# Up matrices of chunks 2 to 4 in seven half-block products, with the third weight sum made by an adding transfer

## The reference

```
h = rmsnorm(x, norm_mix[i]);  x = x + mixer_i(h)
h = rmsnorm(x, norm_mlp[i])
a = relu(h @ w_up)            # 512x1024 @ 1024x4096
x = x + (a * a) @ w_down      # 512x4096 @ 4096x1024
...
return rmsnorm(x, norm_final)
```

## Time and profile before

| | |
|---|---|
| median of 3 runs | 1083.18 us (1082.9 to 1083.55) |
| profiled execution | 1082.86 us, its span 1081.1 us |
| granted TensorE clock | 0.997 of full speed |
| PE busy | 1068.0 us, 99% |
| DVE busy | 723.8 us, 67% |
| ACT busy | 508.4 us, 47% |
| POOL busy | 81.5 us, 8% |

### The profile page before, as it was taken

How to read it: one execution, slowest core, us unless ns; L and a number is a source line. 1 busy time by engine, 2 the same in 40 slices (tenths; PEclk the granted TensorE clock), 3 DMA queues, 4 the chain that set the end, 5 groups by cost and what they waited for, 6 DMA issues and landing times.

```text
span 1081.1 us, 13565 instructions
## 1 busy us (share of the span) xinstructions
PE 1068.0 (99%) x5224; PEld 886.2 (82%) x5224; DVE 723.8 (67%) x1221; ACT 508.4 (47%) x839; POOL 81.5 (8%) x143
## 2 busy tenths in 40 slices
PE   9999999999999999999999999999999999999996
PEld 8888888988888888888877777779888888888884
DVE  5886788676576576578426666535775675675687
ACT  6132256663463463466424444326663463463453
POOL 3480000000000000000110000000000000000000
PEclk9999999999999999999999999999999999999998
DMA  7993235235335335310454333152235235235011
GB/s 239 388 376 108 78 80 187 85 79 175 98 78 176 98 77 175 100 40 20 135 164 134 107 93 96 60 233 78 79 82 192 78 79 193 79 78 195 1 40 78
DMA packets 32672, 133.19 MB, mean 123 GB/s; under 512 B 5280, under 2 KB 5408, under 8 KB 26848
## 3 DMA queue, kind: packets, MB, share of 16 engines
q1 hardware_dynamic: 20448, 69.25, 19.2%
q0 software_dynamic: 12160, 63.07, 18.9%
HBM read 113.80 MB, written 10.48 MB: 115 GB/s over the span
## 4 chain that ended last, share of the span: by engine, by line
PE 98%; DVE 1%; ACT 0%; issue 0%; DVEq 0%; POOL 0%; POOLq 0%; ACTq 0%
PE bank L446 31%; PE bank L448 30%; PE bank L447 30%; PE bank L599 2%; PE bank L581 1%; PE bank L566 1%; PE bank L469 1%; PE bank L614 0%; DVE xs L983 0%; ACT big L749 0%; DVE big L1029 0%; DVE w_l L927 0%; PE bank L636 0%; PE bank L632 0%; DVE big L1249 0%
## 5 line engine op out<-in xcount | busy, mean ns | idle before, releaser
L446 PE MATMUL bank<-a_h,w_h 128*128 128x512 f32 (+1 forms) x896 | 337.3, 377 | 0.1
L448 PE MATMUL bank<-a_h,w_l 128*128 128x512 f32 (+1 forms) x896 | 335.2, 374 | 0.0
L447 PE MATMUL bank<-a_l,w_h 128*128 128x512 f32 (+1 forms) x896 | 335.1, 374 | 0.0
L446 PE MATMUL bank<-w_h,hx 128*128 128x512 f32 x568 | 222.0, 391 | 0.0
L448 PE MATMUL bank<-w_h,hx 128*128 128x512 f32 x568 | 221.0, 389 | 0.0
L447 PE MATMUL bank<-w_l,hx 128*128 128x512 f32 x568 | 221.0, 389 | 0.0
L721 ACT ACTIVATE w_h<-raw 128x1024 fp32r<-128x1024 f32 x115 | 121.3, 1058 | 174.9 <-PE bank L448 142.9
L927 DVE TENSOR_TENSOR w_l<-raw,w_h 128x1024 fp32r<-128x1024 f32 x115 | 139.7, 1220 | 92.0 <-PE bank L448 63.1
L446 PEld LDWEIGHTS bank<-a_h,w_h 128*128 128x128 f32 x896 | 168.7, 188 | 32.5 <-issue 3.1
L448 PEld LDWEIGHTS bank<-a_h,w_l 128*128 128x128 f32 x896 | 168.7, 188 | 30.2
L447 PEld LDWEIGHTS bank<-a_l,w_h 128*128 128x128 f32 x896 | 168.8, 188 | 29.8 <-issue 0.2
(11 more groups left out here) (112 smaller groups left out, 806.0 us busy)
## 6 DMA issues: line engine op xcount, KB each, us to landing
raw<-weights SPq DMA_DIRECT2D x116, 512.0 KB, 3.5
big<-blocks POOLq DMA_DIRECT2D x36, 1024.0 KB, 5.1
big<-big POOLq DMA_DIRECT2D x9, 1024.0 KB, 8.0
bias_tiles<-big POOLq DMA_DIRECT2D x8, 624.0 KB, 9.5
big<-bias_tiles POOLq DMA_DIRECT2D x8, 624.0 KB, 4.1
bias_tiles<-bias_rows POOLq DMA_DIRECT2D x48, 64.0 KB, 12.4
big<-x SPq DMA_DIRECT2D x8, 256.0 KB, 4.7
raw<-wave SPq DMA_DIRECT2D x8, 256.0 KB, 5.0
```

What stands on the lines that cost most here:

```text
L446: nc.tensor.matmul(dst, sh, mh, start=start, stop=False, skip_group_check=again)
L447: nc.tensor.matmul(dst, sh, ml, start=False, stop=False, skip_group_check=again)
L448: return nc.tensor.matmul(dst, sl, mh, start=False, stop=stop, skip_group_check=again)
```

## The change

Six of the eight up matrices (chunks 2 to 4 of each MLP) are computed by a new function `up_seven`, in seven products of half blocks. The weight part stays in the array (stationary) and 256 tokens of the activations move, so that the result keeps the features on the partitions. A product is 14/7 = 2 units, each 4 output slices x 2 slices x 3 matmuls of 256 columns. Now 15 matrices of weights go through blocks (`MATRIX`), 1 + 2 x 7.

- The sums of the input's blocks are made once per MLP from `a_h` and `a_l`: `in_sums` on VectorE in units 5 to 7 of the first up matrix and in products 3 and 4 of the first down matrix, `in_round` on ScalarE, `in_rest` on VectorE in products 2, 5 and 6 of that down matrix. They lie in `sx`, which takes the place of `raw` while no ring unit is in use.
- Results leave by copies and additions of two banks at once (`X_BLOCK`, `c_add`), then relu and square; the activation blocks for the down matrix are summed in whole blocks (`s_block`) and split in whole blocks (`x_block`).
- Down matrices of chunks 2 to 4 take the order P1, P5, P6, P2, P7, P3, P4 (`INNER`; the last one P3 ahead of P7).
- T3 is made by an adding transfer ahead of T4's (`add_sums`); VectorE's third sum goes. `sums_of_y` for the next matrix stands in products 3 and 5 of the one before it.
- Six rooms of 2048 columns hold the four blocks, T2 and a free one in turn (`rooms_of`), and blocks are loaded by SyncE's queue, in one row with the ring's units.
- Outside the end stages, an eviction is one instruction over two banks instead of two.
- The descriptor scratch of GpSimd's transfers is set to 8192.

```diff
-                pool.dma_start(Y21, T2, accum_op=ALU.add).then_inc(t4_in, 16)
+                pool.wait_ge(t_sum, 2 * q + 2)
+                pool.wait_ge(w_split, part_end(q, "P1"))
+                pool.dma_start(room[at["Y11"]], room[at["T2"]], accum_op=ALU.add).then_inc(t3_in, 16)
+                pool.wait_ge(w_split, part_end(q, "P2"))
+                pool.dma_start(room[at["Y21"]], room[at["T2"]], accum_op=ALU.add).then_inc(t4_in, 16)
...
+            def load_matrix(q):
+                before = {at: role for role, at in ROOMS[q - 1].items()}
+                for role in LOAD_ORDER:
+                    was = before[ROOMS[q][role]]
+                    if q == SEQ_ATTN:
+                        sp.wait_ge(pv_done, 2 * KT)
+                    elif was != "free":
+                        sp.wait_ge(w_split, part_end(q - 1, LAST_USE[was]))
...
+                    if was == "T2" and q != SEQ_ATTN:
+                        sp.wait_ge(t3_in, 16 * q)
+                        sp.wait_ge(t4_in, 16 * q)
+                    sp.dma_start(room[ROOMS[q][role]], blocks[q, Y_ROLES.index(role)]).then_inc(y_in[role], 16)
...
+            def up_seven(n, c):                      # TensorE
...
+                for pos, name in enumerate(order):
...
+                    if name in IN_ORDER:
+                        pe.wait_ge(in_lo, 4 * n + IN_ORDER.index(name) + 1)
...
+                    for u in range(2):
+                        w = first + 2 * pos + u
+                        wh, wl = second_form(wh_all, w), second_form(wl_all, w)
+                        pe.wait_ge(w_split, w + 1)
+                        for o in range(4):
+                            f = slice(P * o, P * o + P)
+                            for a in range(2):
+                                k = 2 * u + a
+                                last = three(dst[:, o, :], wh[:, a, f], wl[:, a, f], mh[:, k, :], ml[:, k, :],
+                                             fresh and k == 0 and o % 2 == 0, k == 3, True)
+                        last.then_inc(unit_done, 1)
...
+            def up_seven(n, c):                      # VectorE
...
+                for pos in range(7):
+                    lo(first + 2 * pos + 3)
+                    if pos == 5:
+                        sums_of_y(q + 1, 1)
+                    if pos == 6:
+                        s_block(tc, 0)
+                        s_block(tc, 1)
+                        s_block(tc, 2)
+                        x_block(tc, "P5")
+                    if pos in (1, 4, 5):
+                        dve.wait_ge(unit_done, first + 2 * pos + 2)
+                        c_add(tb, {1: 0, 4: 1, 5: 2}[pos])
+                    if pos == 3:
+                        sums_of_y(q + 1, 0)
+                    lo(first + 2 * pos + 4)
+                    if pos == 2:
+                        x_block(tc, "P4")
+                    if pos == 5:
+                        x_block(tc, "P1")
...
+            def in_sums(n, i):
+                t0, t1 = sum_raw
+                if i == 0:
+                    in_raw(0, "P3")
+                    in_raw(1, "P4")
+                elif i == 1:
+                    nc.vector.tensor_tensor(t1, t0, t1, ALU.add).then_inc(in_sum, 1)
+                    link(nc.vector.tensor_tensor(t0, t0, u_part("P1", False).bitcast(f32), ALU.subtract))
+                elif i == 2:
+                    nc.vector.tensor_tensor(t0, t0, u_part("P1", True).bitcast(f32), ALU.subtract).then_inc(in_sum, 1)
+                elif i == 3:
+                    dve.wait_ge(in_lo, 4 * n + 2)
+                    in_raw(0, "P1")
+                    nc.vector.tensor_tensor(t1, t0, t1, ALU.subtract).then_inc(in_sum, 1)
...
             def second(tc):                          # VectorE
...
                 for pos in range(7 if n is None else 5):
-                    for u in range(2):
-                        if u == 1:
-                            evict(tc, pos)
-                        lo(first + 2 * pos + u + 3)
-                        if (pos, u) == (0, 0):
+                    lo(first + 2 * pos + 3)
+                    if tc in BY_UNIT:
+                        if pos == 0:
                             x_sums(tc, 3)
+                        if tc and pos in (2, 5, 6):
+                            for i in {2: (0, 1), 5: (2,), 6: (3,)}[pos]:
+                                in_rest((tc - 1) // CHUNKS, i)
+                        if tc and pos in (3, 4):
+                            in_sums((tc - 1) // CHUNKS, pos)
+                    elif pos == 0:
+                        x_block(tc, "P6")
+                    elif pos == 1:
+                        x_block(tc, "P2")
+                        s_block(tc, 3)
+                    elif pos < 4:
+                        x_block(tc, order[pos + 2])
+                    if pos == 5:
+                        sums_of_y(seq_of(tc) + 1, 1)
+                    evict(tc, pos)
+                    if pos == 3 and n is None:
+                        sums_of_y(seq_of(tc) + 1, 0)
+                    lo(first + 2 * pos + 4)
```

More of the change, by code:

```diff
@@ L195, in x_part, with up_pair @@
         def x_part(tc, pos, low):
-            at = 2 * D * ((7 * tc + x_index(tc, pos)) % X_SLOTS) + (D if low else 0)
+            if tc in BY_UNIT:
+                slot = (7 * tc + x_index(tc, pos)) % X_SLOTS
+            else:
+                slot = 3 if order_of(tc)[pos] == "P4" else pos % 3
+            at = 2 * D * slot + (D if low else 0)
             return hx[:, at:at + D].rearrange("p (k t) -> p k t", k=4)
-        bank = [ctx.enter_context(nc.psum_tensor(f"bank{b}", [P, 512], f32)) for b in range(8)]
+        banks = ctx.enter_context(nc.psum_tensor("bank", [P, 4096], f32))
+        bank = [banks[:, 512 * b:512 * b + 512] for b in range(8)]
+        def up_pair(name):
+            return block4(banks[:, 512 * UP_BANK[name]:512 * UP_BANK[name] + 1024])
         score, tposed, attn_out = bank[2:4], bank[4:6], bank[6]
@@ L353, in _ @@
+            load_ring(4, W_OUT + 4)
+            load_matrix(1)
+            load_ring(W_OUT + 4, W_OUT + 8)
+            for q in range(2, SEQ_ATTN):
+                load_matrix(q)
+            sp.wait_ge(unit_done, MATRIX[SEQ_ATTN - 1][0])
+            load_ring(W_OUT + 8, W_OUT + 40)
+            load_matrix(SEQ_ATTN)
+            load_ring(W_OUT + 40, W_OUT + 48)
+            for q in range(SEQ_ATTN + 1, N_MATRIX):
+                load_matrix(q)
             for t in range(3):
@@ L540, in mlp @@
+                transposes(norm, 1)
+                unit(up_unit(n, 3), up_bank(n, 3), 0, a_place(norm, 0))
+                for m in range(4):
+                    unit(up_unit(n, m), up_bank(n, m), 1, a_place(norm, 1))
+                for m in range(4, KT):
+                    pe.wait_ge(relu_done, 8 * n + m - 1)
+                    unit(up_unit(n, m), up_bank(n, m))
+                second(1 + CHUNKS * n)
+                for c in range(1, CHUNKS):
+                    up_seven(n, c)
                     second(1 + CHUNKS * n + c)
@@ L1319 @@
     order += [units(w_in, 0, m) for m in range(KT)]
-    order += [units(mlp_w_up[0], 0, m) for m in range(CHUNKS * KT)]
+    order += [units(mlp_w_up[0], 0, m) for m in range(KT)]
     w_v = w_qkv[:, 2 * D:]
@@ L1325 @@
     order += [wide(attn_w_o[0], i, b) for b in range(2) for i in range(4)]
[L1326 removed]
+    order += [units(mlp_w_up[1], 0, m) for m in range(KT)]
     weights = np.stack(order)
     wave = np.stack(order[:4]).reshape(4, P, KT, P).transpose(2, 1, 0, 3).reshape(KT, P, 4 * P)
[L1329 to L1330 removed]
+    sevens = [conv_w_out[0]]
+    for n in range(2):
+        for c in range(CHUNKS):
+            if c:
+                up = mlp_w_up[n][:, D * c:D * (c + 1)]
+                sevens.append(np.concatenate([up[:, 512:], up[:, :512]], axis=1))
+            sevens.append(mlp_w_down[n][D * c:D * (c + 1)])
+    blocks = np.stack([np.stack(quarters(w)) for w in sevens])
     x_tok = x[0].reshape(ROWS, GW, D).transpose(1, 0, 2).reshape(4, P, D)
```

467 lines of the change are left out of this document (324 added, 143 removed).

## The result

The changed kernel takes 1074.39 us (median of 6 runs, 1073.56 to 1075.08), the kernel before beside it 1083.37 us (6 runs, 1082.9 to 1084.08).

The account below looks back on a forecast made before the run. TensorE was taken as the bound, busy 99% of the span. 1082.86 - 19.2 (up matrices) + 12.0 (first down matrices) = 1075.7, plus 0.3 to the runs' median: 1076.0 us; range 1063.5 to 1081.

Parts of the forecast that it names:

- up matrices: Six up matrices, chunks 2 to 4 of both MLPs: 40.3 instead of 43.5 us each, 19.2 us less in all.
- first down matrices: First down matrix of each MLP: VectorE has too much work, TensorE waits 6.0 us in each, 12.0 us in all.
- the start: Stretch up to the matrix behind the convolution; the prediction gave it no term of its own.
- Weight loads: Rival for up matrices in sevens: loads in series, 63.2 us per matrix, 118 us more, about 1201 us; chance 1%.
- wait for the own engine: VectorE operation that must wait for the one before on its own engine: taken to cost 1.25 us.
- two-bank operation: VectorE operation over two banks, not in the earlier trace: taken at 1.2 us, between 1.19 and 1.37.
- operations of VectorE closer together than 1.14 us: Sign of being wrong: VectorE runs its operations closer together than the 1.14 us read from the earlier trace.
- The steady pair: Up matrix in sevens, then inner down matrix: VectorE's work hides, cost nothing, 0.4 us left at the down matrix's unit 2.
- the steady pair is late as well: Rival: 0.5 to 1.2 us late in each of six matrices, 3 to 7 us, 1079 to 1083 us; chance 12%.
- Everything is hidden: Rival: VectorE's extra work never delays TensorE, even in the first down matrices; 1064.0 us; chance 22%.
- The transfers: Adding transfers and block loads: nothing up to a 12 us landing; rival of late adding transfers, 1113 us at 20 us, 8%.
- a chain through a transfer: Sign of being wrong: the chain that ended last passes through a transfer.

Follow-up runs that it names:

- e3: Changed kernel plus one extra 128x1024 VectorE operation at the end of every up matrix in sevens, ahead of the down matrix's unit 2; 1079.27 us.
- e4: Changed kernel with T3 added by VectorE (one 128x2048 operation in product 0) instead of by the adding transfer; 1085.62 us.
- e1: Changed kernel without the sums of the input's blocks, their roundings and remainders, so the output differs; 1064.24 us.
- e6: Changed kernel with e5's moves, and the third input sum moved behind the split of the first down matrix's unit 4; 1063.87 us.
- e2: Changed kernel with the last two input sums, roundings and remainders moved from the first down matrix into the up matrix behind it; 1067.7 us.
- e7: Changed kernel with only the next matrix's first weight sum moved from down product 4 to 5; 1075.68 us.
- e5: Changed kernel with e2's move, and the next matrix's first weight sum moved from down product 4 to 5; 1064.81 us.

## Why the prediction was right

Its mechanism held, and its sizes to 2 us. On the span, -19.1 (up matrices) + 10.0 (first down matrices) + 0.8 (the start) + 0.1 = -8.2, against 1073.0 - 1081.1 = -8.1. The forecast had -19.2 + 12.0 = -7.2. That the profiled execution lies only 1.0 us from it is in part luck: the first down matrices came out 2.0 us cheaper, and the start, which the forecast put at nothing, 0.8 us longer.

- **The up matrices.** 19.2 us were forecast from the slots of the earlier trace rows. The six took 261.1 us before and 242.0 after (40.39 and 40.31 above), so 19.1. By the formula for an isolated gap in the Trainium skill (TensorE: Matmul & The Clock Gate, "Back-to-back issue gap") these matmuls would take 0.109 us and the six matrices would give 28 us, an estimate; the rows of after show 0.120 us and 19.1, and do not agree.
- **Weight loads.** The rival that put them into the path is refuted: 337 loads and 337 matmuls lie in 40.39 us, where the loads alone in series would need 337 x 0.19 = 64 us. A load is still busy for 190 ns in after, longer than the slot of 120 ns in which it is hidden, so the loads overlap the matmuls and one another:

```profile
L588 PEld LDWEIGHTS bank<-a_h,w_h 128*128 128x128 f32 x896 | 170.5, 190 | 20.8 <-issue 6.1
```

- **The first down matrices.** The prediction's 6.0 us each are 5.0. The late units are 4, 10, 12 and 14, as forecast, with 0.4, 1.85, 1.45 and 1.2 us against 0.8, 2.2, 1.5 and 1.5. The 1.0 us less has several small parts. Some 0.3 are there before the stage's surplus begins: lo(3) ended at 234.8, which is 234.0 by the prediction's clock (its stage starts 0.82 us earlier), against 234.3. The pair of sums in unit 6, for instance, started 1.13 us apart (226.56, 227.69), where a wait for the own engine had been charged with 1.25. Another 0.35 is the two-bank operation, five times ahead of unit 14. It was taken at 1.2 us between bounds of 1.19 and 1.37 and follows its neighbour in 1.13, below the lower bound, as any 128x1024 operation does. The last third is spread over the operations between and was not assigned. One of the prediction's own signs of being wrong, operations of VectorE closer together than 1.14 us, is so met by a hair, and this is all that it cost. The two-bank rows:

```profile
L1329 DVE TENSOR_TENSOR xs<-bank,xs 128x1024 f32<-128x1024 f32 x36 | 43.8, 1216 | 12.2 <-issue 12.2
...
L1261 DVE TENSOR_TENSOR big<-bank,big 128x1024 f32<-128x1024 f32 x18 | 22.0, 1225 | 41.0 <-PE bank L590 40.6
```

- **The steady pair.** Costed at nothing, rightly: no wait, 38.11 us. The worked-out end of the split of unit 2, 45.1 us from the up matrix's start, is at 314.88 - 269.74 = 45.14; VectorE ran this with no gap:

```profile
312.52 1.22 DVE L1267 TENSOR_TENSOR hx<-big,hx 128x1024 fp32r<-128x1024 f32 x1
313.66 2.35 DVE L1175 TENSOR_TENSOR w_l<-big,w_h 128x1024 fp32r<-128x1024 f32 x2
```

  e3 measured the margin (0.46 us against 0.4). e4 shows what lies beyond another one, the 1.0 us ahead of lo(5) and lo(6). That makes the rival "the steady pair is late as well" a near miss, 0.5 us away.
- **"Everything is hidden".** 1064.0 us was its price, and e1 (1064.24) and e6 (1063.87) are that case. Its condition, that VectorE be able to start the stage's surplus earlier than its order lets it, was not met; e6 shows that doing part of the work later, behind the stage, serves as well.
- **The transfers.** Rightly costed at nothing for this kernel. GpSimd's lines for T3 (L528) and T4 (L530) and SyncE's for the blocks (L499), each with the times to landing, answer to the earlier trace rows:

```profile
L528 POOL DMA_DIRECT2D big<-big x15: 861/870/979, 137.3 to 1023.7; - x15
...
DMA to landing us min/median/max: 6.9/7.0/9.2
...
L530 POOL DMA_DIRECT2D big<-big x15: 861/870/889, 146.0 to 1040.6; - x15
...
DMA to landing us min/median/max: 6.9/7.7/12.0
...
L499 SPq DMA_DIRECT2D big<-blocks x56: 327/328/1906, 149.8 to 1004.6; - x56
...
DMA to landing us min/median/max: 4.7/4.9/10.3
```

  The largest landing, 12.0 us, is above the 9.2 that the prediction took for the most; it and one of 11.6 stand in the first down matrices, while in the other down matrices of the MLPs T4 landed after 6.9 to 7.7. And the prediction asked only whether T4 lands in time for its own split. What it left out is that a load waits for that landing too, and e2 found the block 1.2 to 1.7 us late once VectorE no longer was.
- **The start.** From the first matmul with `a_h` (near 6.5 us) to the first matmul of the matrix behind the convolution (139 to 141 us) after took 133.7 us and before 132.86. The seven kernels of the experiments, whose code is after's there, took 132.75 to 134.19. Four of these eight have a wait of 0.4 to 0.9 us near 58 us. In after the chain passes here through a load of weights, which lands after 19 us in a stretch in which the DMA engines move 420 GB/s:

```profile
36.84 19.16 DMA raw<-weights
...
56.02 1.07 ACT w_h L908
...
57.11 1.24 DVE w_l L1175
...
58.48 0.47 PE bank L588
```

  Before, ScalarE stands 15.4 us waiting for the same load, its weights are split at 57.50, and TensorE's next start, at 57.65, is 0.3 us late. The prediction names a chain through a transfer as a sign of being wrong. To the letter it is there, but this load is none of the transfers that the change adds, and TensorE waited 0.44 us behind it. With one trace of before, it is not shown whether the change has a part in the 0.8 us; the spread among kernels with the same code there is larger.

## What to carry to other kernels

Once a change frees the bounding engine, lay out the engine that feeds it operation by operation at the stage where it has least slack. The sum over the whole span (75% here) did not show the stage in which VectorE was busy 42.98 of 43.08 us, and within a stage the place in the order decides which unit is late. Work that only a later stage needs belongs in the stage with idle time behind it. Moving one operation within the full stage only moved the wait (e7); once the stage had room, the same move paid (e5). When one lateness is removed, look for what it covered, a load that waited for a landing in this case (e2), and move that as well (e5).

## What the hardware showed that was not expected

- **The clock after a wait.** In e7 TensorE waited 3.11 us, started five more matmuls 0.22 to 0.30 us apart and then went on with starts 0.42 us apart, which is 512 columns at the 1.2 GHz level; the stretch from 819.2 to 822.2 us has a granted clock of 0.71:

```profile
819.22 0.47 PE L588 MATMUL bank<-w_h,hx 128*128 128x512 f32 x1 [3.11 <-DVE w_l L1175]
...
820.45 0.62 PE L590 MATMUL bank<-w_h,hx 128*128 128x512 f32 x1
820.87 0.63 PE L588 MATMUL bank<-w_h,hx 128*128 128x512 f32 x1
821.29 0.63 PE L589 MATMUL bank<-w_l,hx 128*128 128x512 f32 x1
```

  Eight starts of this kind follow one another, then the distance is 0.23 again. The matrix is 0.46 us longer than the one of the first MLP, and the traces show where that comes from. Up to the end of the wait both took 36.35 us. Behind it the slower matmuls took 1.6 us more, and a wait of 1.2 us at unit 14, which the first MLP has, was gone. So the clock is all of the 0.46 us, and VectorE's lateness hid the rest. The first MLP's matrix had a wait of 3.13 us at the same unit, the matmuls after it stayed 0.23 us apart, and its clock is 1.00.

  e4 has two more such waits, of 3.23 and 3.26 us. After both of them TensorE was at the lower level from its first matmul on, for 14 and 7 matmuls, and the clock from 257 to 260 us is 0.50. After waits of 1.64 us or less (after, e3) there was no such fall. So of four waits of 3.1 to 3.3 us three brought the lower level and one did not. What decides between them is open.
- **One two-bank operation is shorter than two of one bank.** VectorE is busy 1216 ns with 128x1024 out of two banks, and 684 with each 128x512. From start to start it is 1.13 us against 1.19. Out of the banks it is no slower than an operation that reads no bank (1216 ns, L1175).
- **Two transfers issued together are both late.** In the first down matrix of the first MLP in after, T4's adding transfer (235.08) and a block load (235.48), 1 MB each, were issued 0.4 us apart and landed after 11.6 and 8.2 us. The second MLP's T4 took 12.0 us, and T4 at these two places in e1 to e3 and e5 to e7 11.2 to 12.3. All the other adding transfers of after landed after 6.9 to 9.2 us, and the median load after 4.9. Which of the two holds up the other was not tried.
